# Input projection of a hybrid attention block: the values' columns first, 128 tokens at a time

## The reference, cut to what matters

```
u    = rmsnorm(x) * pre_norm_w                      # (2048, 1024)
proj = u @ w_in                                     # (1024, 4616): nine blocks of 512 columns and 8 gate columns
sb_q, sb_k, sb_v, sb_z, ml_q, ml_k, ml_v, ml_o, ml_z, ml_i, ml_f = split(proj)
y_sb = head_rmsnorm(stick_breaking_attention(sb_q, sb_k, sb_v)) * silu(sb_z)
qk   = silu(causal_conv(concat(ml_q, ml_k)))
y_ml = head_rmsnorm(sigmoid(ml_o) * mlstm(qk, ml_v, ml_i, ml_f)) * silu(ml_z)
h    = x + rmsnorm(concat(y_sb, y_ml) @ w_out)
out  = h + sigmoid(h @ ple_w_gate + b) * (p @ ple_w_up)
```

## Time and profile before

| | us |
|---|---|
| Median of 3 runs | 1869.4 (1868.65 to 1871.02) |
| The profiled execution, its own time | 1869.05 |
| Its span in the profile | 1867.2 |
| TensorE busy with matmuls | 1778.0 (95%) |
| VectorE, ScalarE, GpSimd busy | 1128.3, 998.2, 694.5 |

### The profile page before, as it was taken

How to read it: one execution, slowest core, us unless ns; L and a number is a source line. 1 busy time by engine, 2 the same in 40 slices (tenths; PEclk the granted TensorE clock), 3 DMA queues, 4 the chain that set the end, 5 groups by cost and what they waited for, 6 DMA issues and landing times. The chain is left out here.

```text
span 1867.2 us, 28230 instructions
## 1 busy us (share of the span) xinstructions
PE 1778.0 (95%) x8972; PEld 1448.1 (78%) x8972; DVE 1128.3 (60%) x1768; ACT 998.2 (53%) x2045; POOL 694.5 (37%) x956
## 2 busy tenths in 40 slices
PE   5999999999789999999999999997799999699998
PEld 4888888878468888888888888885688888588887
DVE  4531213554469888878897888786565665333333
ACT  4421212322257787877777878775777775311111
POOL 2100000000136777777777777776234444100000
PEclk9999999999999999999999999997799999899999
DMA  4657787121294647364846476532445453422221
GB/s 163 167 168 202 227 204 195 50 90 45 96 282 136 201 129 243 109 196 128 231 139 175 153 210 195 155 118 83 154 159 183 155 167 121 156 77 77 76 76 45
DMA packets 193386, 277.13 MB, mean 148 GB/s; under 512 B 66716, under 2 KB 128412, under 8 KB 184184
## 3 DMA queue, kind: packets, MB, share of 16 engines
q1 hardware_dynamic: 189592, 259.95, 45.9%
q0 software_dynamic: 3248, 12.62, 1.9%
q10 hardware_dynamic: 432, 3.15, 0.5%
HBM read 187.41 MB, written 88.26 MB: 148 GB/s over the span
## 5 line engine op out<-in xcount | busy, mean ns | idle before, releaser
L966 PE MATMUL b_late<-w_split,spare 128*128 128x512 f32 x1536 | 436.8, 412 | 1.0 <-ACT b_p_out L1048 0.6
L748 POOL TENSOR_TENSOR b_a_lo<-b_aT,b_a_hi 128x512 fp32r<-128x512 f32 (+1 forms) x320 | 367.0, 1147 | 25.6
L1120 DVE TENSOR_TENSOR_SCAN b_buf<-b_y,b_buf 128x511 f32<-128x511 f32 (+2 forms) x320 | 357.9, 1118 | 9.2
L966 PEld LDWEIGHTS b_late<-w_split,spare 128*128 128x128 f32 x1536 | 265.6, 190 | 43.4 <-issue 1.9
L1130 DVE SCALAR_TENSOR_TENSOR b_buf<-b_buf,b_y 128x512 f32<-128x512 f32 (+2 forms) x320 | 189.2, 591 | 113.7 <-PE b_y L928 111.5
L746 POOL CAST b_a_hi<-b_aT 128x512 fp32r<-128x512 f32 (+1 forms) x320 | 181.8, 568 | 202.7 <-PE b_o L942 156.0
L522 PE MATMUL a_po<-uT_hi,w_split 128*128 128x512 f32 x768 | 241.0, 395 | 2.1 <-DVE w_split L395 2.1
L1034 ACT ACTIVATE b_buf<-b_y 128x512 f32<-128x512 f32 (+2 forms) x320 | 171.3, 535 | 84.9 <-PE b_y L922 83.4
L1025 ACT ACTIVATE b_aT<-b_turned 128x512 f32<-128x512 f32 (+1 forms) x320 | 170.4, 533 | 74.7 <-POOL b_a_lo L748 71.4
L1036 ACT ACTIVATE b_buf<-b_buf 128x512 f32<-128x512 f32 (+2 forms) x320 | 181.9, 568 | 10.2
L904 PE MATMUL b_turned<-b_ident,b_buf 128*128 128x128 f32 x1088 | 172.3, 274 | 1.3 <-ACT b_aT L1025 1.3
(11 more groups left out here) (227 smaller groups left out, 3417.3 us busy)
## 6 DMA issues: line engine op xcount, KB each, us to landing
spare<-u_pair SPq DMA_DIRECT2D x61, 1024.0 KB, 5.4
proj_n<-b_p_out SPq DMA_DIRECT2D x64, 256.0 KB, 5.7
c_gates<-proj_n SPq DMA_DIRECT2D x16, 768.0 KB, 4.5
w_raw<-in_w_in POOLq DMA_DIRECT2D x5, 2048.0 KB, 10.2
x_in<-in_x SPq DMA_DIRECT2D x16, 512.0 KB, 4.2
qk_hi<-stage_hi SPq DMA_DIRECT2D x32, 256.0 KB, 2.6
qk_lo<-stage_lo SPq DMA_DIRECT2D x32, 256.0 KB, 3.2
u_pair<-uT_hi SPq DMA_DIRECT2D x16, 512.0 KB, 4.1
```

The lines of the kernel that those rows point to most:

```text
L748: nc.gpsimd.tensor_tensor(lo[:, cols], raw, hi[:, cols].bitcast(F32), ALU.subtract).then_inc(lo_done, 1)
L966: mm = pe.matmul(late[:], u_in[f % US][:, u_part, k, :], w[:, k, :], start=(i == 0), stop=(i == PASSES - 1))
L1120: nc.vector.tensor_tensor_scan(down, y[u % YS][:, 1:keys][:, ::-1], down, b[:, keys - 1:keys], ALU.add, ALU.subtract).then_inc(log_done, 1)
```

## The change

The values' block goes first, in the form that has tokens in rows, so a product needs one turned tile and not four. `first_tile` runs one tile behind `turn` (`MUL_LAG`), and evacuation and storing run two behind (`READ_LAG`). The first weights are split all at once, after tile 0 was copied. Queries and keys follow in `group`, and all of blocks 1 to 4 are now made transposed. The stores move with their blocks.

The order of the blocks, and the helpers:

```diff
-EARLY = (0, 1, 2, 4, 5)
+EARLY = (2, 0, 1, 4, 5)
...
-        FIRST_SPLITS = (range(0), range(0, 2), range(2, 4), range(4, KT))
+        MUL_LAG, READ_LAG = 1, 2
+
+        def behind(fn, lag, q, j):
+
+            if isinstance(q, int):
+                t = 4 * q + j - lag
+                if 0 <= t < TOK:
+                    fn(t // 4, t % 4)
+            else:
+                fn(q if j >= lag else q - 1, (j - lag) % 4)
```

One step of SyncE:

```diff
-                if isinstance(q, int) and q == TG - 1:
-                    if j < 2:
-                        load_x(q, j + 2)
-                else:
+                if not isinstance(q, int) or 4 * q + j + 2 < TOK:
                     load_x(q, j + 2)
-                if behind(q):
-                    store_first(q, j)
+                behind(store_v, READ_LAG, q, j)
```

One step of ScalarE (VectorE's has `scale` and `low` in place of `square` and `high`):

```diff
                 if has_next(q, j):
                     square(q, j + 1)
-                high(q, j)
-                if behind(q):
-                    first_tile(q - 1, j)
+                if has_tile(q, j):
+                    high(q, j)
+                if isinstance(q, int) and (q, j) == (0, 0):
+                    split(0)
+                if isinstance(q, int) and 4 * q + j - READ_LAG == TOK - 1:
+                    split(1, range(KT - 1))
+                behind(first_tile, READ_LAG, q, j)
```

TensorE: the wait and the form of the first product, and the order:

```diff
-                pe.wait_ge(u_lo_done, 8 * q + (8 + 4))
+                pe.wait_ge(u_lo_done, 8 * q + (2 * j + 2 + 4))
...
-                        mm = pe.matmul(po[j][:], w[:, k, j * P:(j + 1) * P], u[:, k, bass.ds(q * GROUP, GROUP)],
+                        mm = pe.matmul(po[j][:], u[:, k, bass.ds((4 * q + j) * P, P)], w[:, k, :],
...
-                turn(q, j)
-                if behind(q):
-                    first_tile(q - 1, j)
+                if has_tile(q, j):
+                    turn(q, j)
+                behind(first_tile, MUL_LAG, q, j)
...
-            first_group(pe.Fori, step)
-            for j in range(4):
-                first_tile(TG - 1, j)
+            for t in range(TOK + MUL_LAG):
+                step(t // 4, t % 4)
...
-            group(1, True)
-            group(2, False)
-            with pe.Fori(3, GROUPS) as g:
-                group(g, True)
+            with pe.Fori(1, GROUPS) as g:
+                group(g)
```

More of the change, by code:

```diff
@@ L138, in first_group, with has_tile @@
                     step(q, j)
-            for j in range(4):
+            for j in range(4 + READ_LAG):
                 step(TG - 1, j)
-        FIRST_SPLITS = (range(0), range(0, 2), range(2, 4), range(4, KT))
-        def behind(q):
-            return not isinstance(q, int) or q > 0
+        MUL_LAG, READ_LAG = 1, 2
[6 more added lines that the diff above has]
+                fn(q if j >= lag else q - 1, (j - lag) % 4)
         def has_next(q, j):
-            return not (isinstance(q, int) and 4 * q + j == TOK - 1)
+            return not isinstance(q, int) or 4 * q + j < TOK - 1
+        def has_tile(q, j):
+            return not isinstance(q, int) or 4 * q + j < TOK
         def whole_group(fori, evacuate, split_next):
@@ L178, in _ @@
                 ks = slice(n * KT // 4, (n + 1) * KT // 4)
-                pool.dma_start(w_raw[:, ks, :], w_view[:, ks, 0:GROUP]).then_inc(first_w_loaded[n], 16)
+                pool.dma_start(w_raw[:, ks, :], w_view[:, ks, EARLY[0] * GROUP:(EARLY[0] + 1) * GROUP]).then_inc(first_w_loaded[n], 16)
             with nc.allow_non_contiguous_dma("eight gate columns"):
@@ L210, in store_v @@
             def store_v(m, t):
-                i, n = t % 2, m + 2 * TG
+                i, n = t % 2, m
                 rows = bass.ds((m * BANKS + t) * P, P)
@@ L238, in _ @@
             first_group(sp.Fori, step)
-            for j in range(4):
-                store_first(TG, j)
             sp.wait_ge(u_lo_done, 2 * TOK + 4)
@@ L252, in store_u @@
                         .then_inc(u_stored, 16)
-            for m in range(TG):
+            for m in range(2 * TG):
                 for t in range(TG):
-                    store_qk(m + TG, t, slice((m + TG) * P, (m + TG + 1) * P), slice(t * GROUP, (t + 1) * GROUP))
+                    store_qk(m + TG, t, slice(m * P, (m + 1) * P), slice(t * GROUP, (t + 1) * GROUP))
                     if t % 2:
                         store_u(2 * m + t // 2)
[L259 to L263, removed]
             for m in range(2 * TG):
@@ L335, in evacuate_conv @@
                 return tile
-            first_tile = evacuate_hi(0, -SB_SCALE)
+            first_tile = evacuate_hi(0, 1.0)
             def step(q, j):
@@ L341, in step @@
                     square(q, j + 1)
-                high(q, j)
-                if behind(q):
-                    first_tile(q - 1, j)
-            square(0, 0)
[L347 to L356, removed]
+                if has_tile(q, j):
[5 more added lines that the diff above has]
+                behind(first_tile, READ_LAG, q, j)
+            square(0, 0)
+            first_group(act.Fori, step)
+            split(1, range(KT - 1, KT))
+            for g, evacuate in ((1, evacuate_hi(1, -SB_SCALE)),
                                 (2, evacuate_hi(2, 1.0)), (3, evacuate_conv(3)), (4, evacuate_conv(4))):
@@ L429, in convolve @@
                 return tile
-            first_tile = evacuate_lo(0, -SB_SCALE)
+            first_tile = evacuate_lo(0, 1.0)
             def step(q, j):
@@ L435, in step @@
                     scale(q, j + 1)
-                low(q, j)
-                if behind(q):
-                    first_tile(q - 1, j)
-            scale(0, 0)
[L441 to L450, removed]
+                if has_tile(q, j):
+                    low(q, j)
+                if isinstance(q, int) and (q, j) == (0, 0):
+                    split(0)
+                if isinstance(q, int) and 4 * q + j - READ_LAG == TOK - 1:
+                    split(1, range(KT - 1))
+                behind(first_tile, READ_LAG, q, j)
+            scale(0, 0)
+            first_group(dve.Fori, step)
+            split(1, range(KT - 1, KT))
+            for g, evacuate in ((1, evacuate_lo(1, -SB_SCALE)),
                                 (2, evacuate_lo(2, 1.0)), (3, convolve(3)), (4, convolve(4))):
@@ L484, in first_tile @@
                 pe.wait_ge(evacuated[j], q + 1)
-                pe.wait_ge(u_lo_done, 8 * q + (8 + 4))
-                final = isinstance(q, int) and 4 * q + j == 4 * TG - 1
+                pe.wait_ge(u_lo_done, 8 * q + (2 * j + 2 + 4))
+                final = 4 * q + j == TOK - 1
                 for k in range(KT):
@@ L497, in step, with group @@
             def step(q, j):
-                turn(q, j)
-                if behind(q):
-                    first_tile(q - 1, j)
+                if has_tile(q, j):
+                    turn(q, j)
+                behind(first_tile, MUL_LAG, q, j)
             pe.wait_ge(ident_ready, 1)
-            first_group(pe.Fori, step)
-            for j in range(4):
-                first_tile(TG - 1, j)
-            def group(g, transposed):
+            for t in range(TOK + MUL_LAG):
+                step(t // 4, t % 4)
+            def group(g):
                 for m in range(TG):
@@ L516, in group @@
                                 w, u = (w_hi, w_lo)[w_part], (uT_hi, uT_lo)[u_part]
[L517 to L523, removed]
+                                mm = pe.matmul(po[t][:], w[:, k, m * P:(m + 1) * P],
+                                               u[:, k, t * GROUP:(t + 1) * GROUP],
+                                               start=(k == 0 and n == 0), stop=(k == KT - 1 and n == 2))
                             if final and k < KT - 1:
```

2 lines of the change are left out of this document (removed).

## The result

The changed kernel takes 1856.74 us (median of 4 runs, 1854.30 to 1857.65) against 1869.03 us before (1867.64 to 1871.02). The ratio of the runs is 0.9929, with a 95% interval from 0.9917 to 0.9941. It is 12.3 us faster; 1858.4 us was forecast, a gain of 10.6 on the profiled execution. The profiled execution of the changed kernel took 1856.06 us, 13.0 less than that of before.

A forecast was written before the change was run, and what follows sets the result against it. Loading, normalising and splitting bound the stage up to 28.63 us, then TensorE. An earlier first product gains 14.0 us, less 1.7 each for the pitch of blocks 1 and 2: 10.6 off 1869.05 gives 1858.4 us; range 1851.5 to 1863.

The forecast's parts named there:

- The start: First block: first product at 13.6 us, behind the turning of tile 1, and turning of tile 2 at 21.2 us.
- The rise of the clock: First product: clock rises as long after unbroken work starts as before, so turning and product take 9.28 us.
- late-clock rival: First product runs wholly at the lower clock rate: 2.6 us more, 1861.0 us; chance 0.10.
- Tile 2 in time: Ahead of turning 2: square at 15.45, everything the turning waits for ready at 20.0, 1.2 us early.
- The third rival, late turnings: Each of the first steps waits for its tile, 1 to 3 us in all: 1860 to 1862 us; chance 0.09.
- The paced part: First block behind tile 2: 14 steps of 6.38 us and a last product, ending at 116.0; gain so far 14.0 us.
- the slower rival: Stores of values starve the staging buffers in the first block: 32 us more, 1891 us; chance 0.05.
- The pitch of the later blocks: Matmul distance: second block inherits 0.2333 from the first, costing 1.7 us; blocks 3 and 4 stay as before.
- a fifth part of 0.25: Part of the pitch rival (chance 0.25, distance hangs on neither operand, 1855.0 us) where blocks 3 and 4 quicken too: 1851.6.
- the time is given back: Wait at the start of attention, or a slower clock later, grows by the start's gain: about 1868 us; chance 0.06.

The follow-up runs named there:

- the kernel before and its variant: Variant: the kernel before with the values' block multiplied with the weights stationary, leaving out the values' layout; 1865.87 us (ratio 0.9985).

## Why the prediction was right, and where it was off

**The start.** Foreseen: first product at 13.6, turning 2 at 21.2 without a wait. Measured 13.95 and 21.57. The offset is turning 1, which came at 12.36 and not at 11.94: its tile landed 0.4 us later (square at 8.24 in place of 7.82). In the twelve other profiles that turning came between 11.9 and 13.5 us, in the kernel before and its variant (11.9 to 13.3) as in the new order. The lags of 1, 2 and 4 show that this term is the cause of the gain, and the start of the second block followed the sum within 1.5 us.

**The rise of the clock.** 9.28 us from turning 1 to turning 2 were carried over from before, and 9.21 were measured. The late-clock rival did not occur. That the two agree so closely is luck: the rise is not fixed to the work, and with the same code in this stretch turning 1 to 2 took 8.0 to 9.1 us in other profiles.

**Tile 2 in time.** Foreseen 1.2 us of slack, measured 0.7. ScalarE's part was right to 0.01 us (15.44); the rest is one small GpSimd instruction that took 1.01 us and not 0.2, beside VectorE's splitting. The prediction had put the eight splittings ahead of the square on ScalarE and had not asked what VectorE's do to GpSimd. In all ten profiles of the new order this instruction, started between 16.6 and 17.6 us, ended 0.05 us behind VectorE's last splitting, whether that made it 0.43 us long or 1.96. The longest one, in the run with wide value stores:

```profile
13.88 4.90 DVE L387 TENSOR_TENSOR w_split<-w_raw,w_split 128x512 fp32r<-128x512 f32 x8
20.70 1.28 DVE L380 TENSOR_TENSOR uT_lo<-a_pt,uT_hi 128x512 fp32r<-128x512 f32 x2
...
16.86 1.96 POOL L197 TENSOR_TENSOR a_mean_eps<-a_mean_sq,a_eps 128x1 f32<-128x1 f32 x1 [5.42 <-ACT xn L283]
```

So the end of VectorE's splitting, not the square, sets when tile 2 is ready: `uT_lo` of tile 1 was done 3.2 us behind it in all ten. (In the kernel before, beside four splittings, the instruction took 0.59 us and ended 0.05 us behind the third of them; so that it goes on to the last is shown for the new order alone. Why it is held is not shown.) The third rival, late turnings, did not occur in the changed kernel's profile. But the tight place has no margin to rely on: in the run with wide stores `uT_lo` was done at 21.98, 0.45 us behind the start of turning 2, the turning took 1.16 us in place of 1.04, and the step 6.60 us in place of 6.48; with the queries' block `u`-stationary it took 6.58.

**The paced part.** 6.48 us a step, as for 0.2333, and 117.96 for "about 118". The stores cost nothing, as the wide ones show; the slower rival needed transfers of 11.5 us or more to landing, and their median was 3.0.

**The pitch of the later blocks: the step that failed.** The 1.7 us for the first block were right. For the second block, "I take 1.7, since the only block that followed such a one without a stall kept its pitch" was wrong, and so was "Blocks 3 and 4 had it before (one as cause, one as heir), so they stay": all three ran at 0.229. That is 1.7 us less cost and 3.5 us of gain, 5.2 us against the sum. The text named the 3.4 us of blocks 3 and 4 as possible, but its only chance for them (a fifth part of 0.25) went with a first block at 0.229 too, and that block ran at 0.2333. The case that came, the first block slow and all others quick, had no chance of its own. The run with the values' block in the other form shows that both slow blocks before went with the form of that block; why the fourth followed it there, in both profiles, and no block does so in the changed kernel or in its variant with two such blocks, stays open.

**What was not foreseen.** A low rate behind the stall, 1.6 us, and 0.75 us more at the start of attention. The second is the rival "the time is given back" in small, and it goes with the change: the wait there was 17.2 to 18.4 us in all eight profiles with a lag of 1, and 16.55 to 16.9 in the five of the kernel before, its variant and the lags of 2 and 4. Why is not shown. Together with the late turning and the longer stall these took 2.9 of the 5.2 us that the pitch gave above the sum, so it is partly luck that 1858.4 lies so near to the time: 14.0 - 1.7 + 3.5 - 0.2 - 1.6 - 0.75 - 0.3 for the late turning is 13.0.

## What to carry to other kernels

A first product should ask for as few of the tiles that are still being made as its layout allows: choosing which block goes first, and which operand is stationary, can shorten the fill of a pipeline by several steps while the paced part stays nearly as it is (6.48 us a step and 6.38 here). The gain can be summed before anything is run: the start of the first product, the steps behind it, the last product; and a lag is an easy thing to vary to check the sum. A short wait of the bound engine can cost more than itself, so look at the distance of the matmuls behind it as well. And when work is bunched on one engine, look at what the other engines do at that time: here it was a 128x1 instruction of GpSimd that ate most of the slack.

## What the runs showed of the hardware

- Two distances between 128x512 matmuls at the same granted clock of 1.00: 0.2289 and 0.2333 us, 1.9% apart. With the activations stationary it was 0.2333 in every profile. With the weights stationary it was 0.2289 but for three stretches: the fourth block of the kernel before (two profiles of two), one product of its first block, right behind the rise of the clock (one of the two), and the fifth block behind the stall in one profile of the changed kernel. The cause is open.
- Behind a wait of 2.05 to 2.25 us the matmuls fell to 0.43 us apart for about 3 us in four of nine profiles with that stall (both kernels among them) and not in the others; it cost 1.6 us. The fall came 0.9 to 1.6 us after TensorE was at work again, not in the wait: the first matmuls behind it were 0.23 us apart.
- The same at the start: after work at the upper level and a wait of 3.35 us TensorE went on at the upper level for 0.5 us and then fell to the lower one.
- A 128x1 TENSOR_TENSOR of GpSimd that started while VectorE split weights (128x512 TENSOR_TENSOR) ended 0.05 us behind VectorE's last one, in ten profiles of ten, and took 0.43 to 1.96 us where its other fifteen of the stage take 0.19 or 0.20.
- 256 B pieces cost DMA time (share 0.66 against 0.48 for the same bytes), and TensorE's first block took the same time (96.4 and 96.5 us).
